# One entry of an address table per channel tile: in the first stage of a macaron decoder kernel, only tile 0's low half lies 32 bytes off, tiles 1 to 15 lie 128 bytes off

## What is computed

```python
D_MODEL, SEQ, N_META = 2048, 256, 16
D_FF = 5632

def _rmsnorm(x, g):
    xf = x.astype(jnp.float32)
    r = lax.rsqrt(jnp.mean(xf * xf, axis=-1, keepdims=True) + EPS)
    return (xf * r).astype(x.dtype) * g

def _swiglu(x, wg, wu, wd):
    return (jax.nn.silu(x @ wg) * (x @ wu)) @ wd

h = x + 0.5 * _swiglu(_rmsnorm(x, norm_ffn1), w1g, w1u, w1d)      # first stage
u = _rmsnorm(h, norm_mix)
b_gate, c_gate, v, z_pool, g_conv, g_pool = split(u @ w_in)
y_conv = (b_gate * conv3(c_gate * v)) @ w_conv_out
y_pool = (pooled(z_pool) per group @ w_pool_group) * pool_scale
h = h + (sigmoid(g_conv) * y_conv + sigmoid(g_pool) * y_pool) @ w_o
h = h + 0.5 * _swiglu(_rmsnorm(h, norm_ffn2), w2g, w2u, w2d)      # last stage
y = _rmsnorm(h, norm_final)
```

## Time and profile before

| what | value |
|---|---|
| median of 3 runs | 2774.24 us (2774.22 to 2774.65) |
| the profiled execution's own time | 2774.16 us |
| its span, first to last instruction | 2772.3 us |
| granted TensorE clock, mean | 0.998 |
| first stage, start of its first matmul to that of the pool stage | 18.00 to 980.32 us |
| busy in the span | TensorE matmul 2757.8 us, VectorE 1537.4, ScalarE 1052.8, GpSimd 12.4 |
| read from HBM | 408.42 MB, 149 GB/s with the writes |

### The profile page before, as it was taken

One profiled execution on the slowest core, in us unless ns is written; L12 is line 12 of the kernel. 1 busy time (PEld: TensorE's weight loads), 2 busy tenths in 40 slices (PEclk: granted clock), 3 DMA queues, 4 the chain that ended last, 5 costly groups with the idle time before them and its releaser, 6 DMA issues.

```text
span 2772.3 us, 47809 instructions
## 1 busy us (share of the span) xinstructions
PE 2757.8 (99%) x18725; PEld 2754.3 (99%) x18725; DVE 1537.4 (55%) x2166; ACT 1052.8 (38%) x1283; POOL 12.4 (0%) x22
## 2 busy tenths in 40 slices
PE   9999999999999999999999999999999999999998
PEld 8999999999999999999999999999999999999998
DVE  6555455554555585555555555575555555555555
ACT  5333333333333453333333334363333333333334
POOL 0000000000000000000000000000000000000000
PEclk9999999999999999999999999999999999999999
DMA  6444444444444445444444444454444444444443
GB/s 198 152 145 144 139 149 144 144 144 144 144 145 144 143 136 153 152 148 143 158 141 159 152 151 144 151 159 152 152 151 151 151 151 151 151 151 151 151 151 106
DMA packets 347876, 412.27 MB, mean 149 GB/s; under 512 B 13039, under 2 KB 283503, under 8 KB 347446
## 3 DMA queue, kind: packets, MB, share of 16 engines
q1 hardware_dynamic: 347264, 410.24, 46.9%
q0 software_dynamic: 560, 1.32, 0.2%
HBM read 408.42 MB, written 3.32 MB: 149 GB/s over the span
## 4 chain that ended last, share of the span: by engine, by line
PE 98%; ACT 1%; DVE 0%; issue 0%; DMA 0%; SPq 0%; ACTq 0%; DVEq 0%
PE bank L433 33%; PE bank L434 33%; PE bank L435 32%; DMA acc<-in_x_sample 0%; ACT tb L742 0%; PE bank L686 0%; ACT w_hi L702 0%; SPq L338 0%; DVE w_lo L957 0%; DVE tok L1029 0%; DVE xn_lo L1010 0%; ACT h L761 0%; DVE h L1126 0%; PE bank L660 0%; ACT acc L783 0%
## 5 line engine op out<-in xcount | busy, mean ns | idle before, releaser
L957 DVE TENSOR_TENSOR w_lo<-raw,w_hi 128x1024 fp32r<-128x1024 f32 x772 | 944.0, 1226 | 1021.9 <-ACT w_hi L702 1021.1
L702 ACT ACTIVATE w_hi<-raw 128x1024 fp32r<-128x1024 f32 x772 | 815.6, 1059 | 1322.3 <-PE bank L435 1321.3
L433 PE MATMUL bank<-xn_hi,w_hi 128*128 128x320 f32 (+2 forms) x4224 | 1314.3, 311 | 2.7 <-DVE xn_lo L1010 2.7
L435 PE MATMUL bank<-xn_hi,w_lo 128*128 128x320 f32 (+2 forms) x4224 | 1304.4, 309 | 0.0
L434 PE MATMUL bank<-xn_lo,w_hi 128*128 128x320 f32 (+2 forms) x4224 | 1303.4, 309 | 0.0
L433 PEld LDWEIGHTS bank<-xn_hi,w_hi 128*128 128x128 f32 x4224 | 793.0, 188 | 3.2 <-issue 3.1
L435 PEld LDWEIGHTS bank<-xn_hi,w_lo 128*128 128x128 f32 x4224 | 792.2, 188 | 0.0
L434 PEld LDWEIGHTS bank<-xn_lo,w_hi 128*128 128x128 f32 x4224 | 792.2, 188 | 0.0
L435 PE MATMUL bank<-hid_hi,w_lo 128*128 128x320 f32 (+1 forms) x1952 | 606.4, 311 | 0.0
L434 PE MATMUL bank<-hid_lo,w_hi 128*128 128x320 f32 (+1 forms) x1952 | 604.7, 310 | 0.0
L433 PE MATMUL bank<-hid_hi,w_hi 128*128 128x320 f32 (+1 forms) x1952 | 598.9, 307 | 0.4 <-issue 0.4
(11 more groups left out here) (109 smaller groups left out, 493.2 us busy)
## 6 DMA issues: line engine op xcount, KB each, us to landing
raw<-in_w_ffn_gate SPq DMA_DIRECT2D x176, 512.0 KB, 3.5
raw<-in_w_ffn_up SPq DMA_DIRECT2D x176, 512.0 KB, 3.5
raw<-in_w_ffn_down SPq DMA_DIRECT2D x176, 512.0 KB, 3.6
raw<-in_w_in SPq DMA_DIRECT2D x176, 512.0 KB, 3.5
raw<-in_w_conv_out SPq DMA_DIRECT2D x32, 512.0 KB, 3.9
raw<-in_w_o SPq DMA_DIRECT2D x32, 512.0 KB, 3.7
raw<-in_w_pool_group SPq DMA_DIRECT2D x4, 512.0 KB, 4.2
out<-acc SPq DMA_DIRECT2D x8, 256.0 KB, 3.1
```

The costliest lines, as they stand in the source:

```text
L433: pe.matmul(out, slot_hi(n, col, col + P), hi, start=start, stop=False)
L435: return pe.matmul(out, slot_lo(n, col, col + P), hi, start=False, stop=stop)
L702: act.activation(slot_hi(n), raw[:, n % RAW, :], ACT.Copy).then_inc(hi_done, 1)
L957: dve.tensor_tensor(slot_lo(n), raw[:, n % RAW, :], slot_hi(n).bitcast(F32), ALU.subtract).then_inc(lo_done, 1)
```

## The change

It gives the table one entry per channel tile in place of one per four tiles, and sets the entries of tiles 1, 2 and 3 of the first norm to 32 floats (128 bytes). Tile 0 stays at 8 floats (32 bytes), tiles 4 to 15 stay at 32, norms 1 and 2 stay at zero. The list of instructions of every engine is the same before and after.

```diff
-XL_SHIFT = ((8, 32, 32, 32), (0, 0, 0, 0), (0, 0, 0, 0))
+XL_SHIFT = ((8,) + 15 * (32,), KD * (0,), KD * (0,))
...
         def x_lo(norm, k):
-            at = k * ROW + XL_SHIFT[norm][k // 4]
+            at = k * ROW + XL_SHIFT[norm][k]
             return xn_lo[:, at + first_of(norm):at + T]
```

## The result

| | before | changed |
|---|---|---|
| median | 2774.45 us | 2785.51 us |
| executions | 18, from 2774.07 to 2775.48 | 18, from 2772.41 to 2786.70 |
| the profiled execution, its span | 2774.16, 2772.3 | 2786.17, 2784.4 |

The ratio is 1.0027, 95% interval 1.0019 to 1.0036. It is a mean over two outcomes, and no execution lies between them: five of the changed kernel's executions took 2772.41, 2772.45, 2772.52, 2772.64 and 2773.42 us, thirteen took 2785.30 to 2786.70. The first group is the forecast (2772.5), four of its five within 0.15 us and the fifth 0.9 us above; the second is rival A (2785.8). The median belongs to the second, outside the stated range.

What follows compares the result with a forecast made beforehand. TensorE's matmuls, by the distance between their starts, were taken to bound the kernel. Terms of -1.76 and +0.04 gave -1.72 us, so from the 2774.24 us median the forecast was 2772.52 us, range 2772.0 to 2774.4.

Steps and rivals of the forecast that it cites:

- rival A: First stage: speed depends on a state tile 0 alone does not set; adds 11.6 us, 2785.8 us; chance 0.20.
- What bounds the kernel: TensorE, busy 2757.8 of 2772.3 us; the change acts only through the distance between matmul starts.
- (1): Shift table: entries 1, 2 and 3 of the first norm go from 8 to 32; no DMA, wait or weight chunk moves.
- (3): First projection of the first turn: what tiles 1 to 3 save is lost before a wait, 0.04 us.
- (4): VectorE's writes of `xn_lo` at the new address: 0.03 us at most, costed at nothing.
- (5): What follows: weight slots free earlier, nobody is late next, later stages start 1.72 us earlier.
- (2): First-stage projections: three tiles go from 0.920 to 0.9067 us each, in 44 projections, saving 1.76 us.
- The prediction's own sign of being wrong: The first stage's down product changing its speed at all, or TensorE waits other than the first two pieces growing.
- the place that the prediction gave as deciding: Tile 1's six matmuls after 36.02: taking 0.920 us and not 0.907 would mark rival A.
- Rival B: Tiles 0 to 3 are slow by place, weights in slot 0, not by shift; no change, 2774.2 us; chance 0.03.
- C: Only part of the gain comes: 2773.1 us with tile 1 slow, 2773.5 with the first turn slow; chance 0.07.

Runs made afterwards that it cites:

- the pace set from outside: The changed kernel plus twelve extra matmuls at 8 floats, once, ahead of the second projection of the first turn: 2774.63 us, ratio 1.0001.
- Nine fail: The changed kernel with all tiles at 32 floats and nine extra matmuls at 8 floats, once, ahead of the second projection: 2787.37 us, ratio 1.0046.
- the last four: The changed kernel with tiles 12 to 15 at 8 floats and tiles 0 to 11 at 32: 2775.34 us, ratio 1.0001.

## Why the prediction was wrong

*What bounds the kernel, and that only the distance between starts can move:* right. No wait of TensorE for another engine grew, and no count moved.

*(1), (3), (4), (5):* right as far as they go. The wait for tile 4 is there as before (2.7 us in two), the four writes of `xn_lo` took 562 to 565 ns, nothing else is late. In (3) there was nothing to lose, though: the matmuls of tiles 0 to 3 lasted 3.60 us from first to last start both times (18.00 to 21.60 and 17.79 to 21.39).

*(2), the saving of 0.0133 us in each of three tiles:* this is the step that failed, and not by its size, which is real: four of the five short executions are 1.8 to 2.0 us below the median of before, for a forecast of 1.72, and with the pace set from outside the profile shows 0.92 and 13.60 us to the digit. What failed is the step "I take the whole, since twelve tiles of the same projection show it". It took 0.907 as a price that goes with the address. Those twelve run at 0.907 only while TensorE is in step, and the tiles whose address I changed were what had brought it there: tile 0 alone leaves all 868 other groups at 0.920. The sum put that at nothing; it is the 868 x 0.0133 = 11.6 us that I had worked out under rival A. Measured were 11.1 us up to the pool stage. The prediction's own sign of being wrong, a down product that changes its speed, is there: 3.68 us a chunk in place of 3.62.

*Rival A* was the outcome in 13 of 18, at 2785.30 to 2786.70 against 2785.8, with turns of 88.30 us. It had 0.20. Its account was right but for one step: tile 1 does not stay at 0.920 us. It takes 0.91, and tile 2 at 0.93 falls back, so the place that the prediction gave as deciding would have spoken for the forecast. Three reasons against A were weak, and each could be seen to be:
- "By tile 1 the matmuls are already 0.15 us apart": they were so in a passage, not in a pace. The earlier trace rows show tile 1, then at 8 floats, at 0.91 us, and only tiles 2 and 3 at the steady 0.92 of that address. So the trace of before had a passage of more than six and at most twelve matmuls, and the change leaves six. Nine fail.
- "It gets a new try in each of 43 projections": the tries are not independent. A tile 0 that fails hands the next one the same slow pace, and in the profile all 43 fail alike (0.92, 0.91, 0.93).
- "Once in step the loop goes from shift 32 to 8 and back 42 times without a loss": this is true, and it says that a good pace is kept, not that it is found.

*What no case foresaw:* that both outcomes belong to one program. I read one execution's first projection as the kernel's; the pace behind a pause differs from execution to execution (tiles 5 and 6 of the changed kernel: 1.81 us in one profile, 1.85 in the other). Four tiles at 8, and two, hide that, since they lead to 0.907 from either start; with one tile at 8, or none, the start stays to the end. The short outcome came in 5 of 18 executions of the changed kernel, and in 2 of 12 with all tiles at 32. That one of the two outcomes met the forecast is therefore luck of the start, and the forecast did not know of it.

*Rival B* falls with the last four, where tiles 0 to 3 take 0.907 us, and with none at 8. *C*, a part only, is not seen in any profile, and no execution lies between 2773.5 and 2785.3. The fifth short execution, 2773.42 us, is as long as C with a slow first turn would be (2773.5); it has no profile, and the executions of before scatter by 1.4 us, so the runs do not rule C out for it.

What is open: what inside TensorE or the memory the three paces are, whether the other engines' work beside it has a part in keeping one, and what picks one behind a pause. The runs show when the paces change, not why.

## What to carry to other kernels

Where a loop runs at one pace over several addresses, look for the same address at another pace elsewhere in the trace, above all behind pauses, before taking its pace as a price per instruction; if there is one, the slow-looking part may be what sets the pace of the rest. Count how many instructions the passage from one pace to the other takes, and leave that many. And time such a kernel in many executions, since a single execution, or a median, shows only one of its outcomes.

## What the runs showed of the hardware

- Six matmuls (two triples of 336 columns, low pass 32 floats off) take 0.907, 0.920 or 0.933 us with the same instructions and addresses, the mean granted clock being 0.998 or 0.999 in every profiled execution. That is 151.1, 153.3 or 155.5 ns a matmul. The rule of the Trainium skill weighed in the prediction (page "TensorE: Matmul & The Clock Gate", section "Wait — 56ns, not 53.3ns?") has one distance for a number of columns; the runs do not agree with it here. The steps are 6.7 ns per triple, which is 16 columns at 2.4 GHz, my estimate from these rows.
- The paces 0.907 and 0.920 last until something ends them, for over 860 us and ten turns. Behind a pause the pace differs between executions of one program. Another address leads out of 0.920 in some number of matmuls (8 floats: more than nine, at most twelve; 24 floats: six in the one profile that shows it, with the tile behind them still uneven), and a border between addresses can lead into a worse pace (24 floats: 0.907, and 0.933 behind a down product at 32).
- Each address of the low half has paces of its own. Seen over four tiles or more: 8, 16, 40, 48, 0 and 12 floats at 0.920, 56 and 20 at 0.925 (3.70 us for four tiles), 24 at 0.907 and 0.933, 32 at 0.907 and 0.920. At 0.933 tiles at 32 were seen only between two pauses (tiles 5 and 6 before, 1.87 us). For 0, 12, 16, 20, 40, 48 and 56 it is one execution each, so other paces of theirs may not have come up.
